# The sample tokens' attention of a decoder step, moved to GpSimd and VectorE rows during the prompt's attention

## The reference

```
xn = rmsnorm(x);  lru_x, lru_g, q, k, v = split(xn @ w_in)
y_lru = (rg_lru(conv(lru_x)) * gelu(lru_g)) @ w_branch_lru
q, k = rmsnorm per head;  24 heads of 64 in 3 groups (window 128, 512, 2048; step 1, 4, 16)
per group: o, m, l = softmax attention in the window       # prompt: banded; sample: on the cache
o = sum_g l_g exp(m_g - max m) o_g / sum_g l_g exp(m_g - max m);   y_att = o @ w_branch_att
x = x + (g_lru * y_lru + g_att * y_att) @ w_o;   x = x + swiglu(rmsnorm(x)) @ w_ffn
```

```
s_k = q . key_k / 8 + bias_k;   p = softmax(s);   o = sum_k p_k value_k
```

## Time and profile before

| | before |
|---|---|
| median of the runs | 2134.76 us |
| the profiled execution | 2133.12 us, of that 2131.3 us span |
| TensorE busy | 2051.2 us (96%) |
| VectorE, ScalarE, GpSimd busy | 907.5, 548.7, 550.3 us |
| mean granted TensorE clock | 0.974 of full speed |
| prompt's attention, three groups | 618.3 to 1052.2 us |
| `ylru` with the sample's attention | 1052.2 to 1225.1 us |

### The profile page before, as it was taken

The page is one execution under the profiler, slowest core; times in us unless marked ns, Lnnn a source line. Parts: engine busy times, 40 slices in busy tenths (PEclk is TensorE's granted clock), DMA queues, the critical chain, the costliest instruction groups (busy, mean ns, idle before and its releaser), DMA issues.

```text
span 2131.3 us, 33683 instructions
## 1 busy us (share of the span) xinstructions
PE 2051.2 (96%) x13052; PEld 1994.9 (94%) x13052; DVE 907.5 (43%) x1096; ACT 548.7 (26%) x878; POOL 550.3 (26%) x331
## 2 busy tenths in 40 slices
PE   5799899999989999999899999999999999999999
PEld 4799799999979999999899989999999999999999
DVE  8566667677614343323256253433321333213321
ACT  5466634434314443333300011211100011000000
POOL 2222222222211111111112033233233233233232
PEclk9899999999999999999979799999999999999999
DMA  3111112222342423343456162111111111111112
GB/s 127 44 42 42 42 44 87 90 79 90 107 164 94 146 96 140 112 156 107 152 209 236 50 229 89 69 50 39 49 49 40 50 49 39 50 49 40 49 47 92
DMA packets 71404, 188.40 MB, mean 88 GB/s; under 512 B 9258, under 2 KB 28669, under 8 KB 70653
## 3 DMA queue, kind: packets, MB, share of 16 engines
q1 hardware_dynamic: 41392, 136.97, 19.0%
q10 hardware_dynamic: 29964, 50.78, 7.0%
HBM read 145.06 MB, written 45.81 MB: 90 GB/s over the span
## 4 chain that ended last, share of the span: by engine, by line
PE 90%; DVE 4%; DMA 2%; issue 2%; ACT 1%; ACTq 0%; POOL 0%; SPq 0%; DVEq 0%; POOLq 0%
PE ups L466 67%; PE ups L566 12%; PE aux L606 3%; PE ups L585 2%; PE aux L650 1%; PE aux L490 1%; PE aux L628 1%; DMA o_s<-x 1%; PE aux L596 1%; PE aux L517 1%; PE ups L596 1%; DVE ext L1100 1%; DVE big_f L1085 0%; DMA ext<-bt_s 0%; DVE ext L1096 0%
## 5 line engine op out<-in xcount | busy, mean ns | idle before, releaser
L466 PE MATMUL ups<-big,wsp 128*128 128x344 f32 x9360 | 1518.6, 324 | 25.3 <-ACT x L821 5.2
L466 PEld LDWEIGHTS ups<-big,wsp 128*128 128x128 f32 x9360 | 1496.7, 190 | 43.1 <-issue 25.1
L434 POOL CAST wsp<-wraw 128x1024 fp32r<-128x1024 f32 (+2 forms) x160 | 165.2, 1033 | 1526.8 <-issue 696.7
L436 POOL TENSOR_TENSOR wsp<-wraw,wsp 128x1024 fp32r<-128x1024 f32 (+2 forms) x160 | 379.0, 2369 | 12.8
L566 PE MATMUL ups<-big,wsp 128*128 128x344 f32 x1728 | 304.9, 328 | 6.3 <-ACTq L928 6.3
L566 PEld LDWEIGHTS ups<-big,wsp 128*128 128x128 f32 x1728 | 273.5, 190 | 9.7 <-ACTq L928 6.5
L1196 DVE RECIPROCAL x<-x 128x1024 f32<-128x1024 f32 x24 | 157.3, 6553 | 76.2 <-ACT x L887 76.2
L1241 DVE SCALAR_TENSOR_TENSOR x<-ups,ext 128x256 f32<-128x256 f32 (+1 forms) x96 | 52.1, 543 | 206.5 <-PE ups L585 117.5
L1056 ACT ACTIVATE ext<-ext 128x1032 f32<-128x1032 f32 x22 | 23.5, 1067 | 398.9 <-DVE ext L1438 398.9
L1460 DVE TENSOR_TENSOR x<-ups,x 128x1032 f32 x24 | 29.6, 1233 | 213.6 <-PE ups L466 213.6
L1445 DVE TENSOR_TENSOR ext<-ups,ext 128x344 f32<-128x344 f32 x66 | 29.9, 509 | 147.4 <-PE ups L466 147.4
(11 more groups left out here) (192 smaller groups left out, 1229.3 us busy)
## 6 DMA issues: line engine op xcount, KB each, us to landing
wraw<-w_in SPq DMA_DIRECT2D x52, 512.0 KB, 3.4
wraw<-w_ffn_in SPq DMA_DIRECT2D x44, 512.0 KB, 3.2
x<-out_qkv SPq DMA_DIRECT2D x36, 512.0 KB, 4.4
out_qkv<-x ACTq DMA_DIRECT2D x32, 512.0 KB, 3.2
x<-gate_s SPq DMA_DIRECT2D x16, 516.0 KB, 4.2
wraw<-w_merge SPq DMA_DIRECT2D x16, 512.0 KB, 4.8
wraw<-w_ffn_out SPq DMA_DIRECT2D x16, 512.0 KB, 3.5
x<-o_s SPq DMA_DIRECT2D x8, 792.0 KB, 6.5
```

What stands on the lines that cost most here:

```text
L434: nc.gpsimd.tensor_copy(hi, raw).then_inc(w_hi, 1)
L436: nc.gpsimd.tensor_tensor(lo, raw, hi.bitcast(F32), ALU.subtract).then_inc(w_split[slot], 1)
L466: ins = nc.tensor.matmul(ups[:, slot, c, 0:CH], wsp[:, slot, w, k, :], src[:, a, k, c * CH:(c + 1) * CH], start=(k == 0 and w + a == 0), s ...
```

## The change

The sample's attention gets another shape and another place. A row (partition) is one group, head pair and sample: 3 x 4 x 8 = 96 rows.

- In `v`, two transposes bring the sample's raw q and k to rows; they are normed there (ScalarE L906 and L909, VectorE L1218 to L1229 of the new file).
- In `att0` SP first loads the bias rows (12 small transfers), then in each iteration two buffers of 96 x 2048 cached key values (KVB). GpSimd multiplies them by the query (`key_products`), VectorE sums over the head's 64 channels (`key_sums`) at the end of its iteration.
- Between `att0` and `att1` VectorE and ScalarE make the softmax on rows. In `att1` the same happens with values (`value_products`, `value_sums`).
- Between `att1` and `att2` VectorE lays the row results out, and after the first chunk of `ylru` TensorE turns four tiles of them back (`row_parts_turned`). In `ylru` VectorE merges the groups (`row_weights`, `row_output`).
- GpSimd waits for the normed rows before it splits the weights of `att0`, for the softmax before those of `att1`, and for the laid out rows before those of `att2`.
- The two splitting steps of the recurrence's result (L1172, L1173) go from VectorE in `lru` to GpSimd in `att2` (`z_split_tile`), since the free half of that buffer holds the rows until then.
- All caches, the 192 tiny products and the row steps of `ylru` go; ScalarE issues four loads fewer there. Two outputs are stored in place of one.

```diff
@@ sync: the loads @@
+                if name == "att0":
+                    sp.wait_ge(bt_fill, 16)
+                    for g in range(NG):
+                        for f in range(4):
+                            r = 32 * g + NB * f
+                            sp.dma_start(SBI[r:r + NB], bass.AP(tensor=u_s.tensor, offset=(g * HG + 2 * f) * UL + 127,
+                                                                ap=[[0, NB], [UL, 2], [1, P + 1]])).then_inc(row_bias, 16)
                 with sp.Fori(first, iters) as i:
                     for slot in range(2):
                         weights(i, slot)
+                    if name in ("att0", "att1"):
+                        for n in range(2):
+                            if name == "att1":
+                                sp.wait_ge(kv_red[n], i + 5)
+                            else:
+                                sp.wait_ge(kv_red[n], i + 1)
+                            src = A["kr" if name == "att0" else "vr"]
+                            sp.dma_start(KVB[n], src[ds(i * 2 + n, 1)].rearrange("a p n -> p (a n)")).then_inc(kv_ld[n], 16)
...
@@ gpsimd @@
+            def key_products(i, n):
+                pool.wait_ge(kv_ld[n], i * 16 + 16)
+                apart(pool)
+                own = KVB[n].rearrange("p (k c) -> p k c", k=16)
+                q = QKR[:, 0].rearrange("p h e -> p (h e)").unsqueeze(1).broadcast_to([RW, 16, 2 * HD])
+                nc.gpsimd.tensor_tensor(own, own, q, ALU.mult).then_inc(kv_mul[n], 1)
+            def value_products(i, n):
+                pool.wait_ge(kv_ld[n], i * 16 + 80)
+                apart(pool)
+                own = KVB[n].rearrange("p (h e k) -> p h e k", h=2, e=8)
+                for h in range(2):
+                    prob = SC[:, h, 0:P].unsqueeze(1).broadcast_to([RW, 8, P])
+                    ins = nc.gpsimd.tensor_tensor(own[:, h], own[:, h], prob, ALU.mult)
+                ins.then_inc(kv_mul[n], 1)
+            def z_split_tile(i, n):
+                z, hi, lo = big2_f32[:, 0, ds(i * 2 + n, 1), :], big2[:, 1, ds(i * 2 + n, 1), :], big2[:, 0, ds(i * 2 + n, 1), :]
+                apart(pool)
+                nc.gpsimd.tensor_copy(hi, z).then_inc(z_hi, 1)
+                pool.wait_ge(z_hi, i * 2 + (n + 1))
+                apart(pool)
+                nc.gpsimd.tensor_tensor(lo, z, hi.bitcast(F32), ALU.subtract).then_inc(z_split, 1)
+                if name == "att0":
+                    pool.wait_ge(row_q, 1)
+                if name == "att1":
+                    pool.wait_ge(row_exp, 1)
+                if name == "att2":
+                    pool.wait_ge(lru_done, KT)
+                    pool.wait_ge(row_parts, 1)
                 with pool.Fori(first, iters) as i:
                     for slot in range(2):
                         split(name, nk, i, slot)
+                    if name == "att0":
+                        for n in range(2):
+                            key_products(i, n)
+                    if name == "att1":
+                        for n in range(2):
+                            value_products(i, n)
+                    if name == "att2":
+                        for n in range(2):
+                            z_split_tile(i, n)
...
@@ tensor @@
+            pe.wait_ge(sqc_done, 24)
+            for n in range(2):
+                ins = nc.tensor.transpose(aux[0:RW, 1, n * P:(n + 1) * P], sqkv[:, 12 * n:12 * n + 12, :].rearrange("p f b -> p (f b)"), ident[:])
+            ins.then_inc(row_mm, 1)
...
+            pe.wait_ge(row_ev, 1)
...
-            def scores(g):
-                pe.wait_ge(kv_ld[g % 2], 16 * (g // 2 + 1))
-                pe.wait_ge(sm_dve, 2)
-                nc.tensor.matmul(aux[0:ROWS, 1, 400 + g:401 + g], pm[:, 64 * g:64 * g + 64], ones[:, 0:1], start=True, stop=True)
-                for f in range(4):
-                    for b in range(NB):
-                        at = 64 * g + 16 * f + 2 * b
-                        ins = nc.tensor.matmul(aux[0:NKEY[g], 1, at:at + 2], kc[g][:, b, f, :], qm[:, at:at + 2], start=True, stop=True)
-                ins.then_inc(kv_used[g % 2], 1)
...
+            def row_parts_turned():
+                pe.wait_ge(row_parts, 1)
+                for n, part_of in enumerate((ORF, MXF, SUF, POF)):
+                    ins = nc.tensor.transpose(aux[:, 1, n * RW:(n + 1) * RW], part_of, ident[0:RW, 0:RW])
+                ins.then_inc(row_mm, 1)
-            pe.wait_ge(lru_done, KT)
+            pe.wait_ge(z_split, KT)
...
-            scores(0)
-            y_chunks(6, 7)
-            turn(1)
...
+            row_parts_turned()
+            for n, at in enumerate((4, 7, 10, 12, 15, 18, 20, 23)):
+                y_chunks(done, at)
+                turn(n)
+                done = at
+            y_chunks(done, 24)
...
@@ scalar @@
+                if n == 2:
+                    act.wait_ge(row_mm, 1)
+                    nc.scalar.activation(QKR.rearrange("p a h e -> p (a h e)"), aux[0:RW, 1, 0:2 * P], ACT.Copy).then_inc(row_ev, 1)
+                if n == 3:
+                    act.wait_ge(row_sq, 1)
+                    nc.scalar.activation(SST[:, 0:4], SST[:, 0:4], ACT.Sqrt, scale=1.0 / HD, bias=epst[0:RW]).then_inc(row_rt, 1)
+                if g == 1:
+                    act.wait_ge(row_max, 1)
+                    for h in range(2):
+                        ins = nc.scalar.activation(SC[:, h, :], SC[:, h, :], ACT.Exp, bias=SST[:, 6 + h:7 + h], accum_out=SST[:, 8 + h:9 + h])
+                    ins.then_inc(row_exp, 1)
+                    act.wait_ge(sqc_done, 36)
+                    act.dma_start(O["krow"], QKR[:, 1].rearrange("p h e -> p (h e)")).then_inc(out_done, 16)
+                    act.dma_start(O["sv"], sqkv[:, 24:36, :]).then_inc(out_done, 16)
...
+            act.wait_ge(row_mm, 2)
+            nc.scalar.activation(small[:, 0:4 * RW], aux[:, 1, 0:4 * RW], ACT.Copy).then_inc(row_ev, 1)
...
@@ vector @@
-                step.step(nc.vector.tensor_tensor(U, H, GE, ALU.mult))
+                step.step(nc.vector.tensor_tensor(big2_f32[:, 0, ds(i, 1), :], H, GE, ALU.mult))
                 dve.sem_inc(z_done, 1)
-                step.step(nc.vector.tensor_copy(big2[:, 0, ds(i, 1), :], U))
-                step.step(nc.vector.tensor_tensor(big2[:, 1, ds(i, 1), :], U, big2[:, 0, ds(i, 1), :].bitcast(F32), ALU.subtract))
...
+            dve.wait_ge(row_rt, 1)
+            step.step(nc.vector.reciprocal(SST[:, 0:4], SST[:, 0:4]))
+            step.step(nc.vector.tensor_tensor(qk_rows, qk_rows, SST[:, 0:4].unsqueeze(2).broadcast_to([RW, 4, HD]), ALU.mult))
+            for a in range(2):
+                ins = nc.vector.tensor_tensor(QKR[:, a], QKR[:, a], GR[:, a * HD:(a + 1) * HD].unsqueeze(1).broadcast_to([RW, 2, HD]), ALU.mult)
+            ins.then_inc(row_q, 1)
...
+            def key_sums(i, n):
+                dve.wait_ge(kv_mul[n], i + 1)
+                apart(dve)
+                to = SC[:, :, ds(i * 32 + 16 * n, 16)].rearrange("p h k -> p k h")
+                nc.vector.tensor_reduce(to, KVB[n].rearrange("p (k h e) -> p k h e", k=16, h=2), AX_X, ALU.add).then_inc(kv_red[n], 1)
+            def value_sums(i, n):
+                dve.wait_ge(kv_mul[n], i + 5)
+                apart(dve)
+                nc.vector.tensor_reduce(OR[:, :, ds(i * 16 + 8 * n, 8)], KVB[n].rearrange("p (h e k) -> p h e k", h=2, e=8), AX_X, ALU.add)\
+                    .then_inc(kv_red[n], 1)
+            def row_softmax():
+                dve.wait_ge(row_bias, 16 * 4 * NG)
+                for n in range(2):
+                    dve.wait_ge(kv_red[n], 5)
+                step.step(nc.vector.scalar_tensor_tensor(SC[0:64, :, 0:P], SC[0:64, :, 0:P], SCALE, SBI[0:64, :, 1:P + 1][:, :, ::-1], ALU.mult, ALU.add))
+                step.step(nc.vector.scalar_tensor_tensor(SC[64:RW, :, 0:64], SC[64:RW, :, 0:64], SCALE, SBI[64:RW, :, 2:P + 1:2][:, :, ::-1], ALU.mult, ALU.add))
+                step.step(nc.vector.memset(SC[64:RW, :, 64:P], NEG))
+                step.step(nc.vector.scalar_tensor_tensor(SC[:, :, P], SC[:, :, P], SCALE, SBI[:, :, 0], ALU.mult, ALU.add))
+                step.step(nc.vector.tensor_reduce(SST[:, 4:6], SC, AX_X, ALU.max))
+                nc.vector.tensor_scalar(SST[:, 6:8], SST[:, 4:6], -1.0, None, ALU.mult).then_inc(row_max, 1)
+            def row_parts_out():
+                dve.wait_ge(out_done, 64)
+                for n in range(2):
+                    dve.wait_ge(kv_red[n], 9)
+                for to, src in ((ORF, OR), (MXF, SST[:, 4:6].unsqueeze(2).broadcast_to([RW, 2, HD])),
+                                (SUF, SST[:, 8:10].unsqueeze(2).broadcast_to([RW, 2, HD])), (POF, SC[:, :, P:P + 1].broadcast_to([RW, 2, HD]))):
+                    ins = nc.vector.tensor_copy(to.rearrange("p (h e) -> p h e", h=2), src)
+                ins.then_inc(row_parts, 1)
...
+                if g == 1:
+                    row_softmax()
+                if g == 2:
+                    row_parts_out()
...
```

(43 more changed lines are left out.)

222 lines of the change are left out of this document (49 added, 173 removed).

## The result

The changed kernel took 2194.62 us (median of 4 runs, 2193.75 to 2199.87), the kernel before beside it 2134.24: a ratio of 1.0276 with a 95% interval of 1.0259 to 1.0293, 60 us slower. The forecast was 2181, the range 2145 to 2212. The execution that was profiled is the slowest of the four, 2199.87 us, so its trace has to explain 67 us and not 60.

The account below looks back on a forecast made before the run. Prediction: TensorE bounds the prompt's attention, so only added waits cost; `ylru` holds removable sample work. Losses 78 + 12 + 10 + 10 + 4 = 114, gain 68: 46 slower, 2179 us profiled, 2181 beside the median, range 2145 to 2212.

Parts of the forecast that it names:

- `ylru`: Stage `ylru`: without tiny products, transposes and cache loads it takes 105 us against 172.9, a gain of 68 (62 to 72).
- the borders: Six head-pair borders inside `att0` and `att1`: BT lands late behind sums and rows; 13 us each, 78 in all.
- the splitting of z: In `att2`: GpSimd's splitting of the recurrence's result shares time with VectorE's softmax steps; 4 us lost (0 to 10).
- Rival A: Attention borders: SP's new order is hidden, so the kernel gets faster, 2103 us; chance 0.07.
- Start of `att0`: At `att0`'s start: bias transfers and rows stand ahead of VT, QT, KTT and BT; 10 us lost (7 to 15).
- Starts of `att1` and `att2`: Weight splitting waits for the softmax, then for sums and copies: 12 us (10 to 15) and 10 us (8 to 12).
- one of the prediction's own signs of being wrong: In `ylru`: a stage over 115 us, with TensorE waiting for VectorE, would show the forecast wrong.
- rival C: In `ylru`: VectorE bounds the stage, 3 us more in each of eight turns, gain 24 less, 2205 us; chance 0.08.
- Rival B: In `att0` and `att1`: VectorE and GpSimd hold each other up, about 3 us an iteration, 24 us, 2205; chance 0.15.

Follow-up runs that it names:

- The quarter of the rows: Changed kernel with row transfers of 192 KB in place of 768, and one full load of both buffers ahead of `att0`'s weights: 2186.38 us (1.0215).
- the first experiment: Changed kernel with the two row transfers moved behind BT in SP's loop: 2169.2 us (1.0159).
- the second experiment: Changed kernel with bias transfers at the end of `att0`'s loads and GpSimd's three waits moved from ahead of the splits (`att2`: splitting z) to ahead of the products: 2169.12 us (1.0154).

## Why the prediction was right, and where it was short

The mechanism was the one forecast, and the size came out low: the sum had 2179 us for the profiled execution, which took 2199.87. Of these 21 us `ylru` makes 11, the starts of `att0`, `att1` and `att2` 9 and the borders 4; a term that was put too high, the splitting of z, hides 4.

- **The borders.** Forecast 13 us, measured 82.2 / 6 = 13.7. The sums were put at 2.29 us and took 2.27; the first scores were put 17.0 us behind the last copy and came 18.0 behind it (743.62 less 725.58); the rate, 350 GB/s, was 335 in the stand; the 21 matmuls, put at 5.11, took 5.62. By the Trainium skill's 436 GB/s ("DMA: Bandwidth & Descriptors", section "Anatomy of one DMA — SWDGE (gpsimd) path") a border would have cost 10.3 us, an estimate from that figure: the full engines of the stand bear out the lower rate here. But the prediction is wrong that no stretch of the trace of before reaches 436. The earlier trace rows do not, yet in its `ylru` the engines moved 456 GB/s from 1069 to 1073 us and 428 from 1066.5 to 1074.5. The 350 was thus one of several rates seen with full engines, and that the border's lies near it was not derived. The quarter of the rows shows that the bytes count about as the sum had them (2.7 us for 3.4).
- **Rival A** fell as priced: SP's order is not hidden. But the prediction thought of one wait only, that of TensorE for VT to BT; the first experiment shows a second wait, for the store of `o_s`, just behind it. That store's bytes stand in the sum (0.54 MB), but not that VectorE waits for its end. The order of time of the kernel before had this line at the border of the earlier trace rows, and it was not among the prediction's rows:

```profile
708.01 0.42 DVE L1241 SCALAR_TENSOR_TENSOR x<-ups,ext 128x256 f32<-128x256 f32 x1 [8.05 <-DMA o_s<-x]
```

  VectorE's first step came 2.3 us behind the scores (705.68 in the earlier trace rows) because of the store. VectorE already waited for that store before the change, so whatever delays the store delays VectorE.
- **Start of `att0`.** Right in size (12.0 for 10), half wrong in cause: the bias transfers delay the weights and not VT, and the 1.57 MB of rows cost nothing there, since the second experiment keeps them ahead of VT and has 14.2 us, less than the 15.1 of before.
- **Starts of `att1` and `att2`.** 15.4 and 13.7 for 12 and 10, 0.4 and 1.7 above their upper bounds. For `att1` the mechanism is as told:

```profile
831.18 4.48 DVE L1236 TENSOR_REDUCE big_f<-big_f 96x2048 f32 x2
...
837.47 0.17 DVE L1255 TENSOR_SCALAR big_f<-big_f 96x2 f32<-96x2 f32 x1
...
838.95 1.04 POOL L436 CAST wsp<-wraw 128x1024 fp32r<-128x1024 f32 x1 [42.05 <-ACT big_f L929]
...
842.53 5.31 PE L616 MATMUL ups<-big,wsp 128*128 128x344 f32 x24 [10.24 <-POOL wsp L438]
...
850.42 0.93 PE L635 MATMUL ups<-x 64*128 64x128 f32 x8 [1.62 <-DMA ext<-bt_s]
```

  The first piece comes 11.4 us behind the last copy (842.53 less 831.14), where the sum had 11. Behind the pieces TensorE waits once more, 1.6 us for BT, which SP issued behind the rows: that wait was not in the sum. From `att1` to `att2` the waits before the first pieces and the slow matmuls behind them were not taken apart.
- **Splitting z on GpSimd**: 4 us forecast, none measured; the low end (0) held.
- **`ylru`** gained 57 and not 68; this term was the most mis-sized one, outside its 62 to 72. With it one of the prediction's own signs of being wrong came true, if only just: `ylru` over 115 us (115.8), with TensorE waiting for VectorE. The forecast had 1.6 us of wait for the first block and 4 of lag; TensorE waited 6.6, 2.3, 2.5 and 1.5 us for blocks, 12.9 in all. The first block is late by VectorE itself:

```profile
1189.11 0.17 DVE L1347 TENSOR_TENSOR x<-x 128x8 f32<-128x8 f32 x1 [15.58 <-DMA x<-o_s]
...
1192.49 1.04 POOL L436 CAST wsp<-wraw 128x1024 fp32r<-128x1024 f32 x1 [14.13 <-DMA wraw<-w_branch_lru]
1192.56 1.51 DVE L1365 TENSOR_TENSOR x<-x 128x512 f32<-128x512 f32 x1
1193.61 2.66 POOL L438 TENSOR_TENSOR wsp<-wraw,wsp 128x1024 fp32r<-128x1024 f32 x1
1194.11 2.71 DVE L1363 TENSOR_TENSOR x<-x 128x512 f32<-128x512 f32 x1
...
1197.73 1.11 PE L674 MATMUL aux<-ident,x 128*128 128x128 f32 x4 [6.58 <-DVE x L1368]
```

  The block took 8.6 us and not 5.7, for two of its steps ran beside GpSimd's splitting (1.51 and 2.71 us, each 0.69 alone), and its load landed 7 us after the issue. From 1190.90 to 1205.00, in this stand and just behind it, the mean granted clock was 0.69 and then 0.59, and the 24 chunks took 96.7 us of matmuls in all, not 90.7. Part of rival C, then: VectorE sets the pace of some turns, and the later turns took 5 us of it back.
- **Rival B** was not what happened in the changed kernel: there VectorE's small steps were stretched to 2.05 us at most, and at the border shown VectorE had nothing to do while the products ran (734.30 to 743.93; its next step is at 745.42). There are two products an iteration, not the four of 4.6 us that the prediction's sum counts. The mechanism is real all the same: about 1.2 us in three periods of the version with the sums in the middle, and one step of 6.64 us in the experiment that waits for the store. The rule of the Trainium skill ("SBUF — State Buffer", section "Who interferes with whom") that the holder of the shared ports keeps them for its whole instruction fits these ends: the step ends when a product does. It does not say why the step of 6.64 us got no turn between its two products.

The median is 60 us up where the profiled execution is 67; which of the terms is smaller in the other executions no trace here shows.

## What to carry to other kernels

When work is moved beside a well filled stage, ask at which moment of its period its transfers run, not only on how many GB/s the stage leaves free: two thirds of the DMA engines' time was free here (share 0.34 in the earlier trace rows), and the six borders cost 82 us with the rows moving in them and 2 us with the rows in the middle. When one late transfer is mended, look for the next consumer that was just in time before; a store which frees a buffer counts as well as a load. A wait put at the head of an in-order queue holds everything that stands behind it: place it directly ahead of what needs it.

## What the runs showed that was not expected

- A store of 528 KB on ScalarE's queue took 12.3 us in place of 5.2 when 1.6 MB were issued on SP's queue at the same moment: another queue is no cover.
- A VectorE step on two elements per partition (0.17 us) lasted 6.64 us beside two GpSimd products of 4.5 us each, that is until the second one ended and not only the one that was running.
- The same change, with its sums moved to the middle of VectorE's list, three waits and the bias transfers moved and eight turns laid to another pace, goes from 2.8% slower to 3.0% faster (0.9698, 0.9682 to 0.9714) than the kernel before.
